# Even layer of a two-block kernel: norm applied by chunk inside its products, Fourier transforms between their groups, a ring of four mixed chunks

## The chip, the cores and the metric

The kernel runs on one core of one Trainium2 chip. The metric is the device time of one execution in microseconds; the time before is the median of three runs.

## What is computed

The reference chains two blocks of two layers each over 512 tokens of width 1024. The first block (attention, convolution, pooling, FFN) is not touched. The second block has an even layer, then an odd one; both also carry 256 context tokens, so that a row of activations is 768 wide here. What matters of the even layer, cut from the reference:

```python
hl = rmsnorm(xl, norm_pre[layer]) * (1.0 + scale_l) + shift_l      # 512 tokens
hc = rmsnorm(xc, norm_pre[layer]) * (1.0 + scale_c) + shift_c      # 256 context tokens
def proj(h, shift_fn):
    u = h @ w_in                                                   # 1024 -> 3840 columns
    s, gate_r, four, gate_f = split(u, ...)                        # 2560, 768, 256, 256
    s = s + (shift_fn(s) - s) * mu                                 # mixed with neighbours
    ...
yr = (...recurrence over s..., normed) * silu(gate_r)
yf = fourier_mix(four) * silu(gate_f)                              # fft2 over tokens and channels, real part
out = concatenate([yr, yf]) @ w_out
```

## The kernel before

All activations lie channel by channel: a tensor of width 1024 is eight chunks of 128 partitions, 768 tokens wide. A product in full precision takes both operands as a rounded part and a rest (`hi`, `lo`) and makes three matmuls per chunk (`hi·hi`, `hi·lo`, `lo·hi`), each for 256 and for 512 tokens. The column tiles of `w_in` are 30, each 128 wide (512 KB); tiles 0 to 19 are the mixed ones (18 for the recurrence, two for its small projections, called lora), 20 to 25 the gates of the recurrence, 26 and 27 the input of the Fourier mix, 28 and 29 its gates. One "group" is one tile's 48 matmuls into one of four PSUM regions.

Work is cut in stages: `stage` (L174) opens one block in which every engine has its own program, joined by semaphores, and all engines meet at its end. `Products` (from L507) is the helper of a products stage: SyncE loads weight tiles into a ring of three (L545), ScalarE makes `hi` of a tile (L565), GpSimd its `lo` (L596, the first two by VectorE), TensorE issues group after group (L1194), and `hi` and `lo` have two places each, so that tile i+2 can be rounded only when group i is done. `Ahead` lets the stage before load and split the first tiles.

The even layer (`even_layer`, L1916) runs through these stages, none of which overlaps another:

- `second_block` (L3431) loads `kept` (coefficients, 184 KB) and `xc` (context, 1 MB) and waits for both (L3441, L3442).
- `rms_norm` (L1839, by `norm_in`): ScalarE squares (L1855), TensorE sums in strips (L245), `Deviation` (L287 to L293, L253) turns the sums into the inverse root for all rows, VectorE scales (L1883), ScalarE applies gain and shift (L1863).
- `split_chunks` (L1204) makes the two parts of the normed chunks (L1212, L1218), then `serial` makes seven small tables `mus` (L1936, L1938).
- The products stage (L1950 to L1996), which starts with no weights on the chip: 30 groups in tile order by `over_tokens`, which takes all chunks for 256 tokens and then all for 512. ScalarE evacuates a group into `raw` (two places, L1945) or `gated` (L1947). VectorE mixes a raw chunk with its neighbours in seven steps (L1988, L1993) into `u`, which has all 20 chunks; ScalarE's queue sends each to HBM (L1974), and evacuating chunk m waits until chunk m-2 is mixed.
- `fourier` (L2015): loads its three tables (2.7 MB, L2030 to L2032) and waits; 12 channel products in plain fp32 (L2042), each evacuated by ScalarE (L2058) in turn with two banks; then for each of two parts the token products (L2050) and the product with the gate (VectorE, L2064).
- A stage sends the eight gate chunks to HBM (3 MB, L2002) and waits for it.
- `rwkv` (L2339) begins with a stage that loads lora, masks, small weights and the first r, k, v triple (L2367 to L2371), fills `reset`, and applies tanh to lora (L2384). Then `first_terms` (L2530) computes the terms of the first head pair with nothing beside it (L2388 the first projection), and the passes of the recurrence follow.

The odd layer's head is built in another manner, which the prediction's steps read: `residual_and_sums` (L2972) has its first weight tile loaded ahead, and `odd_products` (L3029) applies the norm chunk by chunk (L3160, L3124, L3128, L3163 and, for odd chunks, GpSimd at L3098) while TensorE takes two groups at a time through `multiply_part` as the chunks come (L3103 to L3106). `over_chunks` (L2787) is the order of matmuls used there: per chunk 256 tokens and then 512 (L2795).

## Time and profile before

| | us |
|---|---|
| median of three runs (3401.00 to 3408.59) | 3406.09 |
| the profiled execution's own time | 3404.41 |
| its span, first to last instruction | 3402.6 |
| TensorE busy | 2992.8 (88% of the span) |
| VectorE, ScalarE, GpSimd busy | 1924.0, 1167.4, 1104.5 |
| mean clock granted to TensorE | 0.939 of 2.4 GHz |

The page's busy shares are averages over all layers. The touched part lies between about 1805 and 2163 us of the span: it is read from windows of that stretch, and from timelines of single engines. In a timeline row the square bracket holds the idle time before the row and what ended it; rows that merge several instructions run from the first start to the last end, and xN counts them. A plain fp32 matmul leaves two rows.

### The profile page before, as it was taken

Reading aid. Unit: us, or ns where it says so; the run is one execution under the profiler, and the core shown is the slowest. Engines: PE = TensorE matmul, PEld = TensorE weight load, DVE = VectorE, ACT = ScalarE, POOL = GpSimd, SP = SyncE. Lnnn points to the kernel's source line nnn. Section 1 sums busy time; section 2 is a strip of 40 time slices with the busy share of each in tenths; the row PEclk is TensorE's granted clock in tenths of the full one; section 3 lists DMA queues with packets and bytes.
Section 4 is the critical chain, followed back from the end, with each engine's and each line's share of the span. In section 5 each row is a group of like instructions: output and inputs, shape, how many; then the busy total and the mean of one; then the engine's idle time right before and its main releaser. Section 6 shows DMA issues by size and latency. Waiting matters only on the chain. (4 is left out here: it accounts for less than half of the span.)

```text
span 3402.6 us, 65305 instructions
## 1 busy us (share of the span) xinstructions
PE 2992.8 (88%) x27816; PEld 2373.9 (70%) x27816; DVE 1924.0 (57%) x2634; ACT 1167.4 (34%) x2098; POOL 1104.5 (32%) x630
## 2 busy tenths in 40 slices
PE   6898988999979898899993998599999996799897
PEld 3675566887757566688772887388888894579635
DVE  3597765884159786588405760366666643353152
ACT  3223444332232344333225221244444433332222
POOL 0241133554324122355430221145445442132202
PEclk8898999999989899999996999799999998799998
DMA  9332132333233212233321331100000003132201
GB/s 365 94 90 56 32 88 68 99 93 90 72 85 94 54 38 82 69 97 95 89 79 52 109 109 58 77 17 22 22 15 10 22 9 124 44 105 81 75 13 50
DMA packets 348457, 250.33 MB, mean 74 GB/s; under 512 B 10573, under 2 KB 321539, under 8 KB 347395
## 3 DMA queue, kind: packets, MB, share of 16 engines
q1 hardware_dynamic: 341180, 232.25, 22.7%
q10 hardware_dynamic: 6980, 13.85, 1.3%
q8 instruction: 222, 3.64, 0.4%
q14 instruction: 75, 0.59, 0.1%
HBM read 223.08 MB, written 17.23 MB: 71 GB/s over the span
## 5 line engine op out<-in xcount | busy, mean ns | idle before, releaser
L596 POOL TENSOR_TENSOR weights_lo<-weights_raw,weights_hi 128x1024 fp32r<-128x1024 f32 (+1 forms) x234 | 593.3, 2536 | 1110.8 <-ACT weights_hi L565 1110.8
L1194 PE MATMUL psum<-moving_hi,weights_hi 128*128 128x512 f32 x1472 | 599.9, 408 | 73.8 <-DVE weights_lo L596 46.1
L1194 PE MATMUL psum<-moving_lo,weights_hi 128*128 128x512 f32 x1472 | 582.2, 395 | 0.0
L1194 PE MATMUL psum<-moving_hi,weights_lo 128*128 128x512 f32 x1472 | 581.3, 395 | 0.0
L1194 PEld LDWEIGHTS psum<-moving_hi,weights_hi 128*128 128x128 f32 x1472 | 281.2, 191 | 186.6 <-issue 60.1
L565 ACT ACTIVATE weights_hi<-weights_raw 128x1024 fp32r<-128x1024 f32 (+2 forms) x250 | 252.9, 1016 | 246.1 <-PE psum L1194 241.2
L1194 PEld LDWEIGHTS psum<-moving_hi,weights_lo 128*128 128x128 f32 x1472 | 281.5, 191 | 60.8
L1194 PEld LDWEIGHTS psum<-moving_lo,weights_hi 128*128 128x128 f32 x1472 | 281.9, 192 | 57.1 <-issue 3.8
L2729 POOL TENSOR_TENSOR second_off<-second_mats,second_masks 128x256 f32<-128x256 f32 x180 | 149.5, 835 | 139.9 <-PE psum L2071 139.9
L1194 PE MATMUL psum<-hn_hi,even_hi 128*128 128x256 f32 (+1 forms) x480 | 162.5, 338 | 27.3 <-DVE even_lo L596 27.3
L2720 DVE TENSOR_TENSOR second_wb<-second_wb,psum 128x512 f32<-128x512 f32 (+1 forms) x180 | 112.3, 631 | 113.7 <-PE psum L2071 112.5
L2071 PE MATMUL psum<-second_wb,second_y 64*64 64x64 f32 x2880 | 167.2, 219 | 0.1
L2795 PE MATMUL psum<-tail_hi,odd_hi 128*128 128x512 f32 (+1 forms) x384 | 143.3, 373 | 27.2 <-DVE tail_lo L2953 15.5
L1194 PE MATMUL psum<-hn_lo,even_hi 128*128 128x256 f32 (+1 forms) x480 | 162.4, 338 | 0.0
L1194 PE MATMUL psum<-hn_hi,even_lo 128*128 128x256 f32 (+1 forms) x480 | 161.9, 337 | 0.0
L744 DVE SCALAR_TENSOR_TENSOR cv<-u,columns,cv 128x512 f32<-128x512 f32 x88 | 154.9, 1760 | 3.1
L596 POOL TENSOR_TENSOR odd_lo<-odd_raw,odd_hi 128x2048 fp32r<-128x2048 f32 x19 | 88.7, 4667 | 208.8 <-ACT odd_hi L565 208.8
L596 POOL TENSOR_TENSOR even_lo<-even_raw,even_hi 128x1024 fp32r<-128x1024 f32 x28 | 67.4, 2407 | 247.9 <-ACT even_hi L565 247.9
L2071 PEld LDWEIGHTS psum<-second_wb,second_y 64*64 64x64 f32 x2880 | 138.9, 135 | 12.6 <-issue 12.3
L1194 PE MATMUL psum<-hidden_hi,weights_hi 128*128 128x512 f32 x352 | 139.7, 397 | 7.5 <-POOL weights_lo L596 7.5
L2071 PE MATMUL psum<-second_y,second_wb 64*64 64x64 f32 x2304 | 143.3, 219 | 0.0
L1735 DVE SCALAR_TENSOR_TENSOR conv<-conv_padded,columns,conv 128x512 f32<-128x512 f32 x120 | 139.2, 1160 | 3.5
(453 smaller groups left out, 6639.3 us busy)
## 6 DMA issues: line engine op xcount, KB each, us to landing
weights_raw<-in_w_up SPq DMA_DIRECT2D x88, 512.0 KB, 3.9
weights_raw<-in_w_in SPq DMA_DIRECT2D x80, 512.0 KB, 3.8
start_ada<-in_ada_w SPq DMA_DIRECT2D x12, 2048.0 KB, 16.8
odd_raw<-in_od_w_in SPq DMA_DIRECT2D x16, 1024.0 KB, 5.6
even_raw<-in_ev_w_in SPq DMA_DIRECT2D x30, 512.0 KB, 4.0
weights_raw<-in_w_down SPq DMA_DIRECT2D x32, 448.0 KB, 3.7
weights_raw<-in_w_o SPq DMA_DIRECT2D x16, 512.0 KB, 3.9
weights_raw<-in_w_down SPq DMA_DIRECT2D x16, 512.0 KB, 4.0
```

Source lines behind the costliest of these rows:

```text
L565: self.nc.scalar.activation(self.ring.hi[i % n][:, a:b], self.ring.raw[:, t % self.ring.landing, a:b], ACT.Identity)\
L596: ops.tensor_tensor(self.ring.lo[i % n][:, a:b], self.ring.raw[:, t % self.ring.landing, a:b], self.ring.hi[i % n][:, a:b].bitcast(F32), A ...
L744: nc.vector.scalar_tensor_tensor(y, x[:, 0:L], col("ffn_w", chunk), y, ALU.mult, ALU.add).then_inc(convolved, 1)
L1194: return nc.tensor.matmul(to, (hi, lo)[which][:, at:at + P], moving(k)[part], start=start and k == 0 and i == 0, stop=stop and k == n_k - ...
L1735: chain.then(nc.vector.scalar_tensor_tensor(conv[:, i, :], padded[:, i, k:k + L], col("conv_w", 2 * k + i), conv[:, i, :], ALU.mult, ALU.add))
L2071: last = nc.tensor.matmul(out[ps, :], lhsT[ps, :], rhs[ps, :], start=start, stop=stop)
L2720: V.tensor_tensor(w_, w_, bank_w(n)[:, :, 0:n_cols], ALU.add).then_inc(w_added, 1)
L2729: G.tensor_tensor(off[:, n % 2, :, :], buf.mats[:, slots(g), 0:CH], over(f"{pre_t}{LEVELS[level]}"), ALU.mult)\
L2795: return nc.tensor.matmul(region[:, a:b], (hi, lo)[which][:, at:at + P], parts[part][:, k, a:b], start=n == 0 and i == 0, stop=n == len(or ...
```

## The change

The layer becomes two stages, `even_sums` and `even_products`, and the recurrence's loading stage is gone.

`even_sums`: no stage waits for `kept` and `xc` any more. SyncE sends `xc`, weight tiles 0 and 1, `kept`, tile 2; ScalarE squares only the 512-token part, VectorE the context part; two weight tiles are split in this stage; the `mus` tables are made here; the inverse root is copied to `stats` in SBUF.

`even_products`: groups go in the order 26 to 29, 0 to 19, 20 to 25, all by `over_chunks`, with three PSUM regions (the fourth pair of banks is the Fourier mix's). The norm is applied chunk by chunk at the head while groups 0 and 1 are taken chunk by chunk. Two channel products of the Fourier mix follow each of groups 4 to 9; the token products follow groups 10 and 12. The mixed chunks go through a ring of four places (the first half of the normed chunks' room; the second half holds `z`) and 18 of them to HBM, lora stays in SBUF and gets its tanh here. Gate chunks are sent to HBM one by one (the Fourier pair together). Masks and small weights of the recurrence load here.

`rwkv` starts with `first_terms`, which now loads the first triple itself and fills `reset`.

```diff
+def even_sums(nc, sq, kept, kept_dram, h, xc, xc_dram, mus, stats, strips, at, psum, common, ahead):
+        def _(sp):
+            sp.dma_start(xc, xc_dram).then_inc(context_landed, 16)
+            for i in range(2):
+                ahead.send(sp, i)
+            sp.dma_start(kept, kept_dram).then_inc(kept_landed, 16)
+            ahead.send(sp, 2)
...
+        def _(pe):
+            for c in range(KD):
+                pe.wait_ge(squared, c + 1)
+                pe.wait_ge(context_squared, c + 1)
+                last = sum_in_strips(nc, dev.sums, common["mean_d"], sq[:, c, :], c == 0, c == KD - 1)
+            last.then_inc(dev.summed, 1)
+            dev.pe(pe)
...
+        def _(act):
+            dev.warm(strips[:, T2 // 4:T2 // 4 + 1])
+            for c in range(KD):
+                S.activation(sq[:, c, CTX:], h[:, c, :], ACT.Square).then_inc(squared, 1)
+                if c == KD - 3:
+                    ahead.hi(act, 0).then_inc(hi_made, 1)
+            ahead.hi(act, 1).then_inc(hi_made, 1)
+            dev.act(act)
+            act.wait_ge(dev.spread, 1)
+            S.activation(by_strip(stats), dev.rstd, ACT.Identity)
...
+        def _(dve):
+            dve.wait_ge(context_landed, 16)
+            for c in range(KD):
+                V.tensor_tensor(sq[:, c, 0:CTX], xc[:, c, :], xc[:, c, :], ALU.mult).then_inc(context_squared, 1)
+            dev.dve(dve)
...
+def even_products(...):
+    groups = [(i, over_chunks(nc, 0, range(KD), parts, SPLIT, P), "act") for i in range(30)]
+        s = Products(..., [(1024 * r + 1024 - T2, T2) for r in range(3)], ahead=ahead)
+        def _(sp):
+            s.load(sp, 0, 5)
...
+            sp.dma_start(seq_table, w["dft_seq"].rearrange("s (c p) f -> p s c f", p=P)).then_inc(tables_landed, 16)
...
+            s.load(sp, 5, 8)
...
+        def _(pool):
+            for c in range(1, KD, 2):
+                pool.wait_ge(rounded, c + 1)
+                nc.gpsimd.tensor_tensor(parts[1][:, c, :], hn[:, c, :], parts[0][:, c, :].bitcast(F32), ALU.subtract).then_inc(rest_pool, 1)
+            s.split_lo(pool)
...
+        def _(pe):
+            for c in range(KD):
+                pe.wait_ge(rest_pool if c % 2 else rest_dve, c // 2 + 1)
+                for g in range(2):
+                    s.multiply_part(pe, g, c, KD)
+            for g in range(2, len(groups)):
+                s.multiply(pe, g)
+                for i in channel_items(g):
+                    if i == 0:
+                        pe.wait_ge(tables_landed, 48)
+                        pe.wait_ge(s.by_act, 2)
+                    if i >= 2:
+                        pe.wait_ge(z_taken, i - 1)
+                    j, t = divmod(i, 6)
+                    PE.matmul(channel_bank(i), gated[:, 6 + j, t * P:(t + 1) * P], ch, start=True, stop=True).then_inc(by_channel, 1)
+                if g in token_after:
+                    j = token_after[g]
+                    pe.wait_ge(z_taken, 12)
+                    if j:
+                        pe.wait_ge(gate_done, j)
...
+        def _(act):
+            for c in range(KD + 1):
+                if c < KD:
+                    for i, span, _ in spans:
+                        act.wait_ge(scaled, 2 * c + i + 1)
+                        S.activation(hn[:, c, span], hn[:, c, span], ACT.Identity, bias=shift[:, i, c:c + 1], scale=gain[:, i, c:c + 1])\
+                            .then_inc(shifted, 1)
+                if c:
+                    act.wait_ge(shifted, 2 * c)
+                    S.activation(parts[0][:, c - 1, :], hn[:, c - 1, :], ACT.Identity).then_inc(rounded, 1)
+            for g in range(len(groups)):
+                if g:
+                    s.split_hi(act, g + 1)
+                act.wait_ge(s.ready, g + 1)
+                m = EVEN_TILES[g]
+                if m < 20:
+                    if m >= 2:
+                        act.wait_ge(mixed, m - 1)
+                        act.dma_start(u_dram[:, m - 2, :], u[:, (m - 2) % 4, :]).then_inc(stored[(m - 2) % 4], 16)
+                    S.activation(raw[:, m % 2, :], s.region(g), ACT.Identity).then_inc(s.by_act, 1)
...
+                for i in channel_items(g):
+                    act.wait_ge(by_channel, i + 1)
+                    S.activation(z[:, i // 6, i % 6, :], channel_bank(i), ACT.Identity).then_inc(z_taken, 1)
...
+                if m == 20:
+                    act.wait_ge(mixed, 20)
+                    S.activation(lora[:, 0, :], lora[:, 0, :], ACT.Tanh)
+                if 20 < m < 26:
+                    act.wait_ge(s.by_act, g)
+                    spill(m - 21, m - 20)
+            act.wait_ge(s.by_act, len(groups))
+            spill(5, 6)
...
+        def _(dve):
+            for m in range(20):
+                dve.wait_ge(s.by_act, mixed_at + m + 1)
+                if 4 <= m < 18:
+                    dve.wait_ge(stored[m % 4], 16 * (m // 4))
...
+                if m in (7, 9):
+                    j = (m - 7) // 2
+                    dve.wait_ge(by_token, j + 1)
+                    V.tensor_tensor(gated[:, 6 + j, :], token_out, gated[:, 8 + j, :], ALU.mult).then_inc(gate_done, 1)
...
 def rwkv(...)
-        with stage(nc, "landed tanh_ready reset_ones") as (block, sems):
...
-                self.loads = self.d == 0 and 0 < self.p < RW_PAIRS
+                self.loads = self.d == 0 and self.p < RW_PAIRS
```

## Rows read from the trace of the kernel before

**Rows 1.** Windows: stretch, length; PE, PEld, DVE, ACT, POOL busy; PEclk; DMA share, GB/s

```profile
1805.40:1850.38 44.98, 7.43 (x136) 3.54 (x137) 19.08 (x34) 24.46 (x44) 0.00 (x0) 0.54 0.21 62
1850.38:2102.47 252.09, 252.09 (x1440) 222.97 (x1440) 130.62 (x141) 51.83 (x59) 67.41 (x28) 0.99 0.28 88
2102.47:2163.01 60.54, 26.49 (x74) 14.40 (x73) 2.70 (x6) 6.29 (x15) 0.00 (x0) 0.73 0.40 152
```

**Rows 2.** Timeline of ScalarE in the even products: start us, us, engine, line, operation

```profile
1868.99 0.81 ACT L1945 ACTIVATE raw<-psum 128x768 f32<-128x768 f32 x1 [6.58 <-PE psum L1194]
```

**Rows 3.** SyncE's timeline, and DMA issues of that stretch: count, size, us to landing

```profile
1807.00 0.34 SPq L3441 DMA_DIRECT2D second_kept<-kept_spill  x1
...
second_xc<-context_spill SPq DMA_DIRECT2D x1, 1024.0 KB, 4.9
```

**Rows 4.** Timeline of TensorE in the odd layer: one chunk's sums in strips

```profile
2963.60 0.87 PE L245 MATMUL psum<-tail_room,table 128*32 128x192 f32 x8 [1.18 <-ACT tail_room L3010]
```

**Rows 5.** Timeline of VectorE from the last sums of the odd norm to its products' head

```profile
2964.53 0.36 DVE L287 TENSOR_SCALAR tail_room<-psum 128x192 f32<-128x192 f32 x1 [1.56 <-PE psum L245]
...
2968.92 1.90 DVE L3160 TENSOR_TENSOR tail_room<-h,tail_room 128x512 f32<-128x512 f32 x3 [2.25 <-PEq L183]
```

**Rows 6.** Timelines of ScalarE and VectorE in the even norm and split, by groups

```profile
1823.12 2.73 DVE L1883 TENSOR_TENSOR second_mixed_in<-second_xc,psum 128x256 f32<-128x256 f32 x8 [0.73 <-PE psum L253]
1823.57 9.68 ACT L1863 ACTIVATE second_mixed_in<-second_mixed_in,second_kept 128x256 f32<-128x256 f32 x16 [2.57 <-DVE second_mixed_in L1883]
...
1833.52 5.97 ACT L1212 ACTIVATE hn_hi<-second_mixed_in 128x768 fp32r<-128x768 f32 x8 [0.27 <-PEq L183]
1834.39 7.04 DVE L1218 TENSOR_TENSOR hn_lo<-second_mixed_in,hn_hi 128x768 fp32r<-128x768 f32 x8 [3.76 <-ACT hn_hi L1212]
```

**Rows 7.** Timeline of TensorE at two starts of odd products

```profile
2972.46 0.80 PE L2795 MATMUL psum<-tail_hi,odd_hi 128*128 128x512 f32 x1 [4.71 <-DVE tail_lo L3163]
...
2977.22 0.39 PE L2795 MATMUL psum<-tail_hi,odd_lo 128*128 128x512 f32 x1
...
3001.43 0.80 PE L2795 MATMUL psum<-tail_hi,odd_hi 128*128 128x512 f32 x1 [2.73 <-POOL odd_lo L596]
...
3004.50 0.40 PE L2795 MATMUL psum<-tail_lo,odd_hi 128*128 128x512 f32 x1
```

**Rows 8.** Timelines of VectorE and GpSimd, the same stretch of the odd layer

```profile
2980.84 8.25 DVE L3166 TENSOR_TENSOR tail_room<-second_xc,tail_room 128x256 f32<-128x256 f32 x8
...
2982.60 4.87 POOL L596 TENSOR_TENSOR odd_lo<-odd_raw,odd_hi 128x2048 fp32r<-128x2048 f32 x1 [0.52 <-ACT odd_hi L565]
```

**Rows 9.** Groups of instructions by form: the split of one even weight tile

```profile
L596 POOL TENSOR_TENSOR even_lo<-even_raw,even_hi 128x1024 fp32r<-128x1024 f32 x28 | 67.4, 2407 | 247.9 <-ACT even_hi L565 247.9
```

**Rows 10.** Timeline of TensorE in products taken by chunk, two chunk starts six apart

```profile
2920.82 0.28 PE L2795 MATMUL psum<-tail_hi,odd_hi 128*128 128x256 f32 x1
...
2927.11 0.28 PE L2795 MATMUL psum<-tail_hi,odd_hi 128*128 128x256 f32 x1
```

**Rows 11.** Timeline of TensorE in the Fourier stage: token products of the first part

```profile
2123.74 1.99 PE L2050 MATMUL psum<-second_dft_ctx,second_z 128*128 128x256 f32 x8 [0.47 <-ACT second_z L2058]
...
2132.44 1.89 PE L2050 MATMUL psum<-second_dft_ctx,second_z 128*128 128x256 f32 x8
```

**Rows 12.** Timelines of VectorE and ScalarE around one mixed chunk

```profile
1895.88 6.03 DVE L1993 SCALAR_TENSOR_TENSOR second_mixed_in<-raw,mus,second_mixed_in 128x255 f32<-128x255 f32 x6
...
1902.35 0.33 ACTq L1974 DMA_DIRECT2D mixed_spill<-second_mixed_in  x1
```

**Rows 13.** DMA issues of whole kernel: count, size, median us to landing

```profile
mixed_spill<-second_mixed_in ACTq DMA_DIRECT2D x20, 384.0 KB, 2.3
second_rkv<-mixed_spill SPq DMA_DIRECT2D x6, 1152.0 KB, 6.2
```

**Rows 14.** Timelines of VectorE and ScalarE in the recurrence's first terms

```profile
2166.87 1.76 DVE L2472 TENSOR_TENSOR_SCAN second_cum<-second_reset,second_sg 128x768 f32<-128x768 f32 x1 [3.25 <-ACT second_sg L2441]
...
2172.80 0.84 ACT L2451 ACTIVATE second_e<-second_cum 128x768 f32<-128x768 f32 x1
```

More of the change, by code:

```diff
@@ L2532, in first_terms, with _ @@
                 terms = Terms(sems, 0)
+                @block.sync
+                def _(sp):
+                    terms.load(sp)
                 @block.tensor
```

373 lines of the change are left out of this document (112 added, 261 removed).

## The prediction, as put on record before the changed kernel ran

> **What bounds the kernel now.** I read the page's shares first, then windows over the touched part, then timelines of single engines. TensorE is busy for 88% of the span, so what is worth finding is time in which it stands still, or work on it that something else sets. The windows cut the layer in three [rows 1]. From the end of the block before (1805.40) to the first product (1850.38) there are 45.0 us in which TensorE works 7.4: loads, norm, split, tables and the first weights come one behind another. From there to 2102.47 it works 252.09 of 252.09 us at a clock of 0.99: this stretch is bound by TensorE alone. From 2102.47 to the recurrence's first instruction at 2163.01 there are 60.5 us with 26.5 of TensorE: tables, Fourier mix, a 3 MB store and a load stage in a row. Group 1 is done just before its evacuation at 1868.99 [rows 2], say 1868.95, so 28 groups take (2102.47 - 1868.95) / 28 = 8.34 us each.
>
> So 105.5 us surround the products. The change puts most of it beside TensorE, but the Fourier products stay TensorE's own work and only move into its busy stretch. The sum has three parts, all against the profiled execution: 3404.41 us, 1.68 below the median of 3406.09; its span is 3402.6, with 1.8 around it.
>
> **Up to the products' stage.** The first load leaves at 1807.0 as before; now it is `xc`, which lands 4.9 us after issue [rows 3]: 1811.9. ScalarE's 512-token squares don't wait for it; VectorE's context squares, of the shape of the context scalings, take about 2.73 / 8 = 0.34 us each [rows 6]. TensorE's sums of one chunk of 768 tokens cost 0.87 us at the low clock [rows 4]; back to back I take 0.75, so eight chunks from 1812.3 end at 1818.0 to 1818.5. That is later than the last square (six squares, `hi` of tile 0 behind its landing at about 1813.5, two squares: 1815.6), so ScalarE's two weight splits hide behind the sums; if the tile lands 3 us later they no longer do, and each further us counts. In the odd layer VectorE's first step behind the sums starts at 2964.53 and its products' head at 2968.92 [rows 5], 4.4 us with the stage's change between. The same steps are here, the `mus` tables fit beside the copy of the root. Head starts at H = 1822.4 (bounds 1821 and 1825).
>
> **The head, groups 0 and 1.** Per chunk ScalarE needs two shifts, 9.68 / 8 = 1.21 us, and one rounding, 5.97 / 8 = 0.75 [rows 6]: 1.96, so 15.7 for eight. VectorE needs 0.63 (1.90 / 3 [rows 5]) and 0.34 per chunk, and 7.04 / 8 = 0.88 for every second [rows 6]: 11.3. GpSimd makes four rests of 768 columns, by width 0.75 of 2.41 us [rows 9]: 7.2. The first chunk is ready after three chunks' scaling, one rounding and one rest, about H + 4.9. TensorE's pace by chunk is 6.29 / 6 = 1.05 us per group [rows 10], 2.10 for two groups, 16.8 for eight chunks at the full clock. It will start at 1.2 GHz: in the odd head that lasted from 2972.46 to 2977.22, where a matmul's row falls from 0.80 to 0.39 [rows 7]: 4.8 us of which half is lost. So group 1 is done at H + 4.9 + 16.8 + 2.4 = H + 24.1 = 1846.5. The last chunk must be there 2.1 us earlier, at H + 22. With all engines side by side it is there at about H + 18.
>
> VectorE and GpSimd don't run side by side freely: eight context scalings took 8.25 us while one `odd_lo` of 4.87 ran [rows 8], against 2.73 for the same shape alone. The Trainium skill, SBUF — State Buffer, section Terms, says why: the two share a port pair that one takes for a whole instruction while the other fully blocks. By that rule the two engines' work adds up, 11.3 + 7.2 = 18.5, plus some 2 of start: the last chunk at H + 20.5. The trace agrees with it, and it speaks against this head: it leaves 1.5 us of room instead of 4.
>
> **The stall behind the head.** Both `hi` places are in use until groups 0 and 1 end, and these now end 1.05 us apart. So tile 2 is rounded only when group 0 is done: evacuation 0.81 [rows 2], `hi` 0.75 x 4 / 3 = 1.0 by width, `lo` 2.41 [rows 9], hand-offs 0.1: 4.3 us, less the 1.05 of group 1: TensorE stands 3.3 us. In the odd products a wait of 2.73 us was followed by half clock from 3001.43 to 3004.50 [rows 7], 1.5 lost; I take 1.5 (bounds 0 and 2.4). Group 2 in effect starts at 1846.5 + 3.3 + 1.5 = 1851.3 instead of 1868.95: **17.6 us less**.
>
> **The middle.** Chunk order: 8 x 1.05 = 8.39 instead of 8.34, 28 times: +1.4. Twelve channel products: 24 rows at 1.99 / 8 = 0.25 us, as plain fp32 rows of that width take [rows 11]: 6.0. Each pair finds both banks taken a group earlier, so no wait. Token products: 2132.44 - 2123.74 = 8.70 us per part [rows 11], 17.4 for two. The second part waits for the first gate product, behind the mixing of chunk 7: one mix ends at 1901.91 and the next group is done by 1902.35 [rows 12], 0.44 us of room, and the gate product is 0.96: 0.5 of stall (0 and 1.5). The tables (2.7 MB) stand in SyncE's queue before tile 5, but are sent some 60 us before group 4's products ask for them. Ring of four: chunk m waits for the store of m-4, sent two groups earlier and landed in 2.3 us [rows 13]; hidden by 16.8 us, and without that cover each group would wait for a landing. Three PSUM regions: an evacuation is done some 1.3 us into the next group, hidden. The SyncE queue's late loads (masks, small weights) have over 150 us. ScalarE gets seven stores, twelve copies of half an evacuation and tanh in a stretch in which it is busy 51.8 of 252 us. Together **+25.3 us**.
>
> **The tail.** Behind the last group: evacuation 0.8, last store landing 2.3 [rows 13], waits and the stage's change 0.6: the recurrence's first stage starts 3.7 us after TensorE, against 60.54 before. In it the triple now loads beside the projection: 6.2 us to landing [rows 13] and some 0.7 of VectorE for `kk` (between the 0.34 and 0.88 of VectorE in [rows 6]), so the scan starts 6.9 after the stage's start instead of 2166.87 - 2163.01 = 3.9. But the exponentials started only at 2172.80 [rows 14], 9.8 after the stage's start, when the scan (1.76) and its difference (0.9) had been done at 6.6: 3.2 us of room for 3.0. I take 0.3 (bounds 0 and 3). **56.5 us less.**
>
> **Sum.** -17.6 + 25.3 - 56.5 = -48.8: 3355.6 for an execution like the profiled one, 3357.3 for the median: **3357**.
>
> **Rivals.**
> 1. *The head is bound by its chunks.* The room of 1.5 us is gone (a rest on GpSimd slower, ScalarE kept by its hand-offs); TensorE stops between chunks and stays longer at 1.2 GHz, where a chunk costs 4.2. For: the blocking in [rows 8]. Against: the odd head, built alike, went to full clock in 4.8 us. Four more chunks at half clock are +8.4, with a late last chunk +10: 3367. Chance 0.15.
> 2. *The Fourier insertions cost waits.* Each of the eight places where TensorE changes between products and Fourier work costs a hand-off of about 1 us (late copy of `z`, gate product behind a late mix): +8: 3365. For: room of only 0.44 us in rows 12. Against: copies of 0.4 against a group of 8.4. Chance 0.10.
> 3. *The gaps close better.* The stall doesn't lower the clock (1.5), `xc` lands sooner when first and alone and the sums run at their narrow shape's rate (2), the gate product waits for nothing (0.5), group 1's tail hides more (2): 3351. Chance 0.14.
> 4. *Slower: mixing sets the pace.* Place: VectorE's loop over 20 chunks, now behind evacuation, ring store and gate product. It decides from 8.39 us per chunk; to lose the whole gain it must take 48.8 / 20 = 2.4 more, 10.8. A store landing more than 16.8 us after issue, or GpSimd's `lo` blocking all of it over again (6.7 + 2.4 = 9.1, not enough), would be wanted; at 11.5 us per chunk the time is 3357 + 20 x 3.1 = 3419. For: the blocking in [rows 8]. Against: the mix already runs beside `lo` and ends within the group [rows 12]. Chance 0.02.
> 5. *The change doesn't do what it says*, that is, the norm or the transforms aren't hidden: the Fourier products never were (they are in the sum), and stages fewer is certain. If the head's overlap failed whole, with loads and norm as long as before, 17.6 is lost: 3374. Chance 0.01.
>
> **How the numbers follow.** The forecast has 0.58. The range takes rivals 1 to 3 in and the bounds of the unknown costs: 3347 (rival 3 with the low ends of the tail and the start) to 3370 (rival 1 with the tail's 3). About 0.2% of 3406, 7 us, is what a measurement of this kernel can tell from no change; only rival 4 comes near or above it: faster 0.97, same 0.01, slower 0.02.
>
> **What would show it.** In the profile after: `stats` copied at about 1822; products' first matmul near 1827, chunk starts 2.1 us apart once the clock is up; one TensorE wait of about 3.3 us on GpSimd's `lo` before group 2; groups 8.4 us apart, 9.3 with channel products, 17.1 with token products; a window of the products stage busy all but 5 us; first terms' first projection 3.7 us behind the last product, at about 2113. I am wrong if group 1 ends after 1855, if mixed chunks are more than 8.5 us apart without Fourier work between, or if the recurrence's passes change in length.

## The result: 1.5% faster, and where the time went

The changed kernel takes 3352.28 us (median of four runs, 3348.69 to 3356.36) against 3403.55 for the kernel before in the same sitting (3399.52 to 3408.59): a ratio of 0.985, 95% interval 0.9835 to 0.9864. Forecast were 3357, range 3347 to 3370. The profiled execution took 3348.69, its span is 3346.9.

| us | before | after |
|---|---|---|
| profiled execution, span | 3404.41, 3402.6 | 3348.69, 3346.9 |
| end of the block before (VectorE's last step, taken as the layer's start) | 1805.39 | 1802.89 |
| from there to the first product | 44.99 | 21.82 |
| to the end of the last product | 297.08 | 305.58 |
| to the recurrence's exponentials, as in [rows 14] | 367.41 | 318.98 |
| from the exponentials to the end of the span | 1229.8 | 1225.03 |
| TensorE busy, clock granted | 2992.8, 0.939 | 2986.4, 0.948 |

The touched layer, by the two marks that both kernels have, is 48.4 us shorter; the sum of the forecast was 48.8. The other 7.3 us of the 55.7 between the two profiled executions lie ahead of the layer and behind it, where nothing was changed; the first experiment asks what they are.

The three parts of the layer changed like this. The first product comes 23.2 us sooner after the layer's start, the stretch of products is 31.7 us longer in place (283.76 against 252.09), and the time from the last product to the exponentials fell by 56.9 us. Before, the latter began with these rows of TensorE:

```profile
2114.16 9.11 PE L2042 MATMUL psum<-second_dft_channels,second_gated 128*128 128x256 f32 x24 [11.68 <-DMA second_dft_ctx<-in_dft_ctx]
...
2163.01 2.90 PE L2388 MATMUL psum<-second_lora,second_w 64*128 64x256 f32 x4 [21.81 <-PEq L183]
```

That is 11.7 us of waiting for the tables, 27.0 from the first Fourier product to the end of the last, and 21.8 of store and loads; 3.9 us are left of it.

Windows of the changed kernel, which answer to [rows 1] (columns as there): up to the first product, the two groups by chunk, the other products with the Fourier work, the end of the stage, the recurrence's first 9.5 us.

```profile
1802.89:1824.71 21.82, 5.96 (x73) 3.67 (x73) 9.23 (x26) 11.81 (x20) 4.67 (x2) 0.58 0.63 180
1824.71:1844.40 19.69, 19.17 (x96) 16.41 (x96) 10.63 (x13) 13.12 (x20) 8.02 (x4) 0.88 0.39 138
1844.40:2108.46 264.06, 260.81 (x1416) 221.81 (x1416) 131.07 (x142) 53.73 (x70) 67.05 (x28) 0.99 0.28 91
2108.46:2112.34 3.88, 0.00 (x1) 0.00 (x0) 0.00 (x0) 0.82 (x2) 0.00 (x0) 1.00 0.50 203
2112.34:2121.87 9.53, 6.69 (x11) 3.12 (x12) 4.48 (x7) 5.10 (x6) 0.00 (x0) 0.52 0.38 124
```

TensorE now stands still for 16 us ahead of its first product, 3.2 inside and 3.9 behind, and works in all the rest. The waits of TensorE between 1820 and 2113, with the total us, the times and the longest:

```profile
PE psum L2716 <- DVE hn_lo L1965: 6.5, 1, 6.5
PE psum L2310 <- PEq L183: 3.9, 1, 3.9
PE psum L2716 <- POOL even_lo L596: 3.2, 1, 3.2
PE psum L1908 <- DVE second_gated L1986: 0.6, 1, 0.6
```

These are the four that the prediction named: the head's first chunk, the change of stage behind the last gate store, the split of tile 2, and the gate product. There is no fifth. The sums stage runs as forecast too; from its timelines (VectorE's context squares, TensorE's sums, the copy of the root, the first step of the head):

```profile
1804.50 0.34 SPq L1789 DMA_DIRECT2D second_xc<-context_spill  x1
...
1809.46 2.77 DVE L1827 TENSOR_TENSOR second_gated<-second_xc 128x256 f32<-128x256 f32 x8 [6.56 <-DMA second_xc<-context_spill]
...
1810.03 5.34 PE L245 MATMUL psum<-second_gated,table 128*32 128x192 f32 x64 [18.63 <-DVE second_gated L1827]
...
1818.30 0.81 ACT L1821 ACTIVATE second_raw<-psum 128x768 f32<-128x768 f32 x1 [2.12 <-PE psum L253]
...
1819.70 0.69 DVE L1962 TENSOR_TENSOR second_mixed_in<-h,second_raw 128x512 f32<-128x512 f32 x1 [1.30 <-PEq L183]
```

The first square on `xc` starts 5.0 us after its load was issued, the sums take 0.67 us a chunk (0.75 forecast), and the head starts 16.8 us behind the block before (17.0 forecast).

What did differ from the forecast stands in TensorE's timeline behind the head:

```profile
1824.71 0.58 PE L2716 MATMUL psum<-hn_hi,even_hi 128*128 128x256 f32 x1 [6.47 <-DVE hn_lo L1965]
...
1847.10 0.58 PE L2716 MATMUL psum<-hn_hi,even_hi 128*128 128x256 f32 x1 [3.22 <-POOL even_lo L596]
...
1852.17 0.63 PE L2716 MATMUL psum<-hn_lo,even_hi 128*128 128x512 f32 x1
...
1853.50 0.40 PE L2716 MATMUL psum<-hn_hi,even_hi 128*128 128x512 f32 x1
...
1858.40 0.28 PE L2716 MATMUL psum<-hn_hi,even_hi 128*128 128x256 f32 x1
```

A matmul of 512 columns has a row of 0.63 us until about 1853 and of 0.40 behind it: 6.1 us at half clock behind the wait. Group 2, from 1847.10 to 1858.40, takes 11.30 us; in two profiles whose clock stays up behind the same wait (gates_at_end and rests_on_dve below) it takes 8.51. So 2.8 us are lost. The term in the sum was 1.5, its upper bound 2.4.

### The profile page after: what moved, and what is told of

Read it like the earlier page. It is cut to its first block and busy times, and to the rows that moved or that the text cites. A ratio compares the mean times of both kernels' runs of the same rounds, so it can differ in the third digit from the quotient of the medians.

```text
span 3346.9 us, 65146 instructions
## 1 busy us (share of the span) xinstructions
PE 2986.4 (89%) x27752; PEld 2368.6 (71%) x27752; DVE 1922.6 (57%) x2636; ACT 1164.4 (35%) x2091; POOL 1115.7 (33%) x636
## 5 line engine op out<-in xcount | busy, mean ns | idle before, releaser
L2716 PE MATMUL psum<-hn_hi,even_hi 128*128 128x256 f32 x480 | 166.7, 347 | 9.7 <-DVE hn_lo L1965 6.5
L2716 PE MATMUL psum<-hn_lo,even_hi 128*128 128x256 f32 x480 | 164.9, 344 | 0.0
L2716 PE MATMUL psum<-hn_hi,even_lo 128*128 128x256 f32 x480 | 163.3, 340 | 0.0
L755 DVE SCALAR_TENSOR_TENSOR h<-h,psum 128x512 f32<-128x512 f32 x16 | 11.0, 688 | 228.4 <-PE psum L1150 228.4
```

What stands on the lines that cost most here:

```text
L755: nc.vector.scalar_tensor_tensor(h[:, m, :], h[:, m, :], ALPHA, s.region(g), ALU.mult, ALU.add).then_inc(s.by_dve, 1)
L2716: return nc.tensor.matmul(region[:, a:b], (hi, lo)[which][:, at:at + P], parts[part][:, k, a:b], start=n == 0 and i == 0, stop=n == len(or ...
```

## How the experiments are read

Medians of one kernel move by 2 or 3 us from one measurement to the next and the intervals are 0.3% wide, so steps of 1 to 6 us are read from the profiles. I take three lengths from each: **layer** (the layer's start to the exponentials), **products** (first product's start to last product's end, with the Fourier work between), and **half clock** (the time in that stretch in which rows have their long form, at the head and behind the wait for tile 2). "Net" is the products less half of their half-clock time. Half is a little too much: a chunk's six matmuls take 1.92 us at half clock (1849.19 to 1851.11 in the changed kernel) and 1.05 at full, so that 0.45 of such a stretch is lost. The last column takes off 0.45.

| kernel | median us | ratio to before | layer | products | half clock: head, behind wait | net | at 0.45 |
|---|---|---|---|---|---|---|---|
| changed | 3352.28 | 0.985 | 318.98 | 283.76 | 4.6, 6.1 | 278.4 | 278.9 |
| after_again | 3352.08 | 0.9851 | 317.95 | 282.95 | 3.6, 5.5 | 278.4 | 278.8 |
| head_order | 3346.69 | 0.9838 | 312.78 | 278.53 | 6.1, 0 | 275.5 | 275.8 |
| hi_first | 3351.60 | 0.9840 | 317.14 | 282.47 | 5.9, 3.4 | 277.8 | 278.3 |
| serial_head | 3363.21 | 0.9880 | 325.86 | 276.75 | 3.1, 0 | 275.2 | 275.3 |
| no_fourier | 3331.76 | 0.9787 | 294.52 | 260.11 | 6.1, 3.5 | 255.3 | 255.8 |
| gates_at_end | 3359.90 | 0.9863 | 321.78 | 280.43 | 3.5, 0 | 278.7 | 278.8 |
| load_stage | 3360.05 | 0.9865 | 324.27 | 283.10 | 5.9, 3.5 | 278.4 | 278.8 |
| token_order | 3351.22 | 0.9845 | 312.58 | 278.51 | 2.7, 0 | 277.1 | 277.3 |
| rests_on_dve | 3348.65 | 0.9838 | 315.46 | 280.34 | 3.2, 0 | 278.8 | 278.9 |
| ring_of_two | 3355.05 | 0.9855 | 320.44 | 284.89 | 4.7, 6.1 | 279.5 | 280.0 |
| all_three | 3347.86 | 0.9836 | 310.98 | 276.01 | 3.6, 0 | 274.2 | 274.4 |
| all_four | 3346.71 | 0.9828 | 310.92 | 275.36 | 4.6, 0 | 273.0 | 273.3 |

Net repeats to 0.1 us in three kernels whose products are the same (changed, after_again, load_stage), to 0.4 with the two others (gates_at_end, rests_on_dve). At 0.45 all five agree to 0.1, so the 0.4 came from the halving.

## Experiments

### The same kernel again

> The changed kernel once more, unaltered. The touched layer is 48.4 us shorter between its marks in the two traces, yet the profiled executions differ by 55.7 and the medians by 51.3. Theory 'the rest is variation from execution to execution' (mine): the ratio comes out between 0.9845 and 0.9865, and in this profile the parts outside the layer that were shorter (first block -2.5 us, recurrence and odd layer together -4.8 us) differ from those of before by other amounts, their sum nearer to -2. Rival 'the change also makes code outside the layer shorter' (other addresses, other DMA timing): the same parts are shorter by the same 7.3 us again, within 1 us.

Measured: ratio 0.9851, 0.9836 to 0.9866. The layer starts at 1804.76 instead of 1802.89, and behind the exponentials the span goes on for 1227.89 instead of 1225.03: the 7.3 us have shrunk to 2.5 (0.6 and 1.9) with nothing changed. Over the thirteen profiles of this case that have the new layer the start lies between 1802.17 and 1809.00, mean 1805.2 (before: 1805.39), and the rest between 1225.03 and 1233.99, mean 1229.6 (before: 1229.8). So the one profile of before lies at the mean of the thirteen, and the 7.3 us were variation of single executions. The rival is out. It also says that a difference of two profiled executions can be off by 7 us in this kernel; the layer between its marks varies by far less.

### The stall behind the head: order of the first two groups

```diff
-            for c in range(KD):
-                pe.wait_ge(rest_pool if c % 2 else rest_dve, c // 2 + 1)
-                for g in range(2):
-                    s.multiply_part(pe, g, c, KD)
+            for g, c in ((0, 0), (1, 0), (0, 1), (1, 1), (0, 2), (1, 2), (0, 3), (0, 4), (1, 3), (0, 5), (0, 6), (0, 7),
+                         (1, 4), (1, 5), (1, 6), (1, 7)):
+                if g == 0:
+                    pe.wait_ge(rest_pool if c % 2 else rest_dve, c // 2 + 1)
+                s.multiply_part(pe, g, c, KD)
```

> Only the order of the parts of groups 0 and 1 at the head changes: group 0 is finished some 4.2 us ahead of group 1, so tile 2 can be rounded and split while TensorE still works. Theory 'the stall behind the head is the split of tile 2, and the half clock after it is a consequence of the stall' (mine): the 3.22 us wait goes to at most 0.3, the clock stays up at 1847 (3.0 us back), some 0.6 us of new waiting for chunks early in the head; -5.8 us against the changed kernel. Rival 'the head is bound by the arrival of its chunks': group 0 alone reaches each chunk sooner, the wait only moves from behind the head into it; 0 to -2 us. Rival 'the clock falls there anyway': the wait goes, the half clock stays, -2.8.

Measured: net 275.5 against 278.4, and no half clock behind the head; layer 312.78 against 318.98 and 317.95, so 5.7 less than their mean; median 5.4 below the unaltered kernel beside it. ScalarE's timeline shows why (evacuation of group 0, then `hi` of tile 2, each twice):

```profile
1842.08 0.81 ACT L1938 ACTIVATE second_gated<-psum 128x768 f32<-128x768 f32 x1 [3.42 <-PE psum L2717]
1842.78 1.05 ACT L565 ACTIVATE even_hi<-even_raw 128x1024 fp32r<-128x1024 f32 x1
1846.28 0.81 ACT L1938 ACTIVATE second_gated<-psum 128x768 f32<-128x768 f32 x1 [2.44 <-PE psum L2717]
1846.98 1.05 ACT L565 ACTIVATE even_hi<-even_raw 128x1024 fp32r<-128x1024 f32 x1
```

Group 0 is evacuated 4.2 us ahead of group 1 instead of 1.65, and the split of tile 2 (4.3 us) fits beside group 1's last chunks. The first rival is out: TensorE has no wait over 0.3 us in the head. The clock did not fall either; one profile says little of that, since the next experiment shows the same wait without a fall, but the clock stays up in all four kernels that lack the wait. The room that the prediction gave to the head was there.

### The size of the wait and the clock: tile 2 rounded ahead of the evacuation

```diff
-                if g:
+                if g > 1:
                     s.split_hi(act, g + 1)
                 act.wait_ge(s.ready, g + 1)
+                if g == 0:
+                    s.split_hi(act, 2)
```

> ScalarE rounds tile 2 before it evacuates group 0 instead of after. Both theories: the wait of 3.22 us behind the head shrinks by one evacuation of 0.8 to about 2.4 or 2.5. Theory 'any wait of that size brings the clock down' (the odd head's wait of 2.73 us was followed by half clock): -0.7 to -1 us against the changed kernel, with half clock for some 4 to 6 us after the wait. Rival 'there is a size of wait between 1.75 and 2.73 us under which the clock stays' : -3.7 us, and full clock after the wait.

Measured: the wait is 2.61 us, net 277.8, 0.6 less. TensorE's rows behind it:

```profile
1848.59 0.39 PE L2718 MATMUL psum<-hn_hi,even_hi 128*128 128x256 f32 x1 [2.61 <-POOL even_lo L596]
...
1849.31 0.63 PE L2718 MATMUL psum<-hn_lo,even_hi 128*128 128x512 f32 x1
...
1852.94 0.39 PE L2718 MATMUL psum<-hn_lo,even_hi 128*128 128x512 f32 x1
```

So the shorter wait was followed by half clock as well, for 3.4 us. But my theory that a wait of this size brings it down each time is wrong. Eight profiles have the same wait of 3.22 us, from the same instruction, between the same groups; the half clock behind it lasted 6.1, 5.5, 3.5, 0, 3.5, 0, 0 and 6.1 us. Windows of 6.0 us from the end of this wait, of the changed kernel, of load_stage, and of gates_at_end (whose edits touch nothing here):

```profile
1847.10:1853.10 6.00, 6.00 (x19) 5.13 (x20) 0.00 (x0) 0.47 (x1) 2.28 (x1) 0.50 0.60 175
```

```profile
1848.09:1854.09 6.00, 6.00 (x26) 5.26 (x27) 0.00 (x0) 0.47 (x1) 2.28 (x1) 0.72 0.60 175
```

```profile
1850.51:1856.51 6.00, 6.00 (x35) 5.29 (x36) 0.00 (x0) 0.47 (x1) 2.29 (x1) 1.00 0.61 175
```

ScalarE, GpSimd and the DMA share are alike; the clock is 0.50, 0.72 and 1.00, and TensorE gets through 19, 26 or 35 recorded matmuls. The price of this wait's clock, read from the length of group 2, is between 0 and 2.8 us from one execution to the next, 1.4 on average of the eight.

One thing in the table goes with it: how long the half clock at the head had lasted, which had ended some 15 us before the wait began. In the three of the eight with the shortest (2.7 to 3.5 us) the clock stayed up; in the next three (3.6, 4.6 and 4.7) it was down for 5.5 to 6.1 us; in the two with the longest (5.9 and 6.1) for 3.5, and hi_first, with 5.9, for 3.4. So the two stretches hang together; why, and what sets the first, no experiment here shows. The four kernels without a wait there (head_order, serial_head, all_three, all_four) show full clock.

### What the overlap is worth

```diff
-            for c in range(KD):
-                pe.wait_ge(rest_pool if c % 2 else rest_dve, c // 2 + 1)
-                for g in range(2):
+            pe.wait_ge(rest_pool, KD // 2)
+            pe.wait_ge(rest_dve, KD // 2)
+            for g in range(2):
+                for c in range(KD):
                     s.multiply_part(pe, g, c, KD)
```

> TensorE waits for all eight chunks, then takes group 0 whole and group 1 whole, instead of chunk by chunk. Theory 'overlapping products with the chunks is worth what the chunks take' (mine): the first product comes 14.2 us later; group 0 and group 1 take 16.8 us plus some 2.3 at the low clock; tile 2 is split in the shade of group 1, so that the 3.2 us of wait and the 3.0 us of low clock behind it are gone: +8.1 us against the changed kernel, of which the overlap alone is 14.2. Rival 'the chunks come sooner when TensorE is not beside them': last chunk clearly earlier than H + 19.25, and the result below +6.

Measured: TensorE waits 20.6 us instead of 6.5, the first product comes 35.40 us into the layer instead of 21.82 and 21.30, 13.8 later; net is 3.2 less (3.5 at 0.45), about the stall of 3.22; the layer is 7.4 longer than the mean of the two unaltered profiles (318.5). The last rest ends 19.1 us behind the head's start, as in the changed kernel (19.25), so TensorE's work beside them does not slow the chunks, and the rival is out. The median is 11 us higher; the layer explains 7.4 of the 11, and the rest stays unexplained, though this profile's layer starts late (1809.00, the latest of all).

Of the 23.2 us by which the first product comes sooner than before the change, the overlap is thus 13.8. The other 9.4 (no wait for `kept` and `xc` in a stage of their own, weights loaded and split ahead, the tables `mus` beside other work, fewer stages) are not told apart by any experiment.

### Fourier work left out

```diff
-        channel_items = lambda g: range(2 * (g - 4), 2 * (g - 4) + 2) if 4 <= g < 10 else ()
-        token_after = {10: 0, 12: 1}
+        channel_items = lambda g: ()
+        token_after = {}
...
-                    V.tensor_tensor(gated[:, 6 + j, :], token_out, gated[:, 8 + j, :], ALU.mult).then_inc(gate_done, 1)
+                    V.tensor_tensor(gated[:, 6 + j, :], gated[:, 6 + j, :], gated[:, 8 + j, :], ALU.mult).then_inc(gate_done, 1)
```

> Leaves out the Fourier mix's twelve channel products, the copies of their results and the token products; the gate is multiplied with the untransformed input instead, so that the gate products and stores stay. Theory 'the Fourier mix costs TensorE its own length and nothing besides' (mine): the layer, from the end of the block before to the recurrence's exponentials, is shorter than in the changed kernel by 5.1 for the channel products, 17.2 for the token products and 0.6 for the wait on the gate: -22.9 us, within 0.7. Rival 'the insertions cost hand-offs or slow the mixing': the gain is larger, -25 or more. Rival 'something else is late in their place' (mixing, tile loads): less than 21 us is gained and new waits stand on TensorE.

Measured: net 255.3 against 278.4, 23.1 less, and no new wait. Groups are 8.40 us apart where channel products follow them at 9.25. The Fourier mix costs TensorE its own length; the eight changes between the two kinds of work, which rival 2 of the prediction priced at 1 us each, cost the 0.55 us on the gate product and nothing else.

### Stores and loads in the tail

gates_at_end sends the gates in one store behind the last group:

```diff
-                if m == 10:
-                    act.wait_ge(gate_done, 2)
-                    spill(6, 8)
...
-                if 20 < m < 26:
-                    act.wait_ge(s.by_act, g)
-                    spill(m - 21, m - 20)
...
-            spill(5, 6)
+            act.wait_ge(gate_done, 2)
+            spill(0, 8)
```

> All eight gate chunks go to HBM in one store behind the last group, instead of one by one as they are ready. Theory 'only the last store lies in the open' (mine): the wait between the last product and the first terms grows from 3.9 us to about 10.3, since 3 MB landed 8.7 us after issue in the kernel before against 2.3 for one chunk: +6.4 us, nothing else moves. Rival 'the end of the products stage is bound by something else' (tail of the small loads, the lora's tanh): +3 or less. Rival 'stores beside the products cost them bandwidth': the products stage gets shorter by over 1 us without them.

load_stage gives the first triple a stage again:

```diff
-                self.loads = self.d == 0 and self.p < RW_PAIRS
+                self.loads = self.d == 0 and 0 < self.p < RW_PAIRS
...
+        with stage(nc, "landed") as (block, sems):
+            @block.sync
+            def _(sp):
+                sp.dma_start(rkv[:, :, :], triple(0)).then_inc(sems[0], 16)
+                sp.wait_ge(sems[0], 16)
```

> The first r, k, v triple gets a stage of its own again between the products and the first terms. Theory 'the triple's landing is hidden by the first projections' (mine): 6.2 us to landing and 0.4 for the change of stage come into the open; the scan no longer waits for the triple, but the exponentials then come 9.5 to 9.8 us behind the first terms' start as before: +6.6 us. Rival 'the exponentials are held up by the triple too': the exponentials come earlier in their stage by 2 or 3 us, so the total is +4 or less.

Measured: the wait ahead of the first terms is 10.13 us in gates_at_end and 10.42 in load_stage, against 3.91. TensorE's first row of the recurrence in each:

```profile
2119.22 2.04 PE L2305 MATMUL psum<-second_lora,second_w 64*128 64x256 f32 x3 [10.13 <-PEq L183]
```

```profile
2118.63 2.90 PE L2316 MATMUL psum<-second_lora,second_w 64*128 64x256 f32 x4 [10.42 <-PEq L183]
```

That is +6.2 and +6.5 with 6.4 and 6.6 expected; net is 278.7 and 278.4, so the small stores cost the products nothing that can be seen. In load_stage the scan no longer waits for the triple, yet the exponentials start 9.80 us into the stage, as they did before the change (9.79) and as they do with the triple's load beside them (9.50 and 9.79). VectorE's and ScalarE's timelines of the changed kernel:

```profile
2118.25 0.62 DVE L2392 TENSOR_SCALAR second_kk<-second_rkv,second_kept 128x768 f32<-128x768 f32 x1 [4.64 <-DMA second_rkv<-mixed_spill]
2118.79 1.75 DVE L2394 TENSOR_TENSOR_SCAN second_cum<-second_reset,second_sg 128x768 f32<-128x768 f32 x1
...
2118.92 0.90 ACT L2366 ACTIVATE second_a<-psum,second_kept 128x768 f32<-128x768 f32 x1 [3.01 <-PE psum L2310]
2120.57 0.96 DVE L2398 TENSOR_TENSOR second_e<-second_cum,second_sg 128x768 f32<-128x768 f32 x1
2120.57 1.28 ACT L2373 ACT_TABLE_LOAD   x1
2121.87 0.84 ACT L2373 ACTIVATE second_e<-second_cum 128x768 f32<-128x768 f32 x1
```

The exponentials need the scan and the difference behind it (L2398), which is done at 2121.53. ScalarE is never idle after 2118.92: it comes to them at 2121.87, behind a square and a table load of 1.28 us. So the triple is hidden, with 0.34 us to spare, and 0.33 to 0.68 in all profiles that have its load beside the first terms, against 3.2 without it.

### The order inside a group

```diff
-    groups = [(i, over_chunks(nc, 0, range(KD), parts, SPLIT, P), "act") for i in range(30)]
+    by_chunks = [over_chunks(nc, 0, range(KD), parts, SPLIT, P) for i in range(30)]
+    by_tokens = lambda made: [made[6 * c + 3 * side + i] for side in range(2) for c in range(KD) for i in range(3)]
+    groups = [(i, by_tokens(made) if i > 1 else made, "act") for i, made in enumerate(by_chunks)]
```

> Groups 2 to 29 take all chunks for 256 tokens and then all for 512, as in the kernel before; groups 0 and 1 stay by chunk. Theory 'the order by chunk costs 0.06 us per group' (from 8.40 us between evacuations against 8.34 before): -1.6 us over 28 groups. Rival 'the 0.06 comes from Fourier work, stores and loads beside the products': 0, groups stay 8.40 apart.

Measured: evacuations follow each other in 8.34 us in this kernel,

```profile
2021.45 0.81 ACT L1937 ACTIVATE second_raw<-psum 128x768 f32<-128x768 f32 x1 [6.58 <-PE psum L2718]
2029.79 0.81 ACT L1937 ACTIVATE second_raw<-psum 128x768 f32<-128x768 f32 x1 [6.58 <-PE psum L2718]
```

and in 8.40 in the changed one:

```profile
2024.87 0.81 ACT L1935 ACTIVATE second_raw<-psum 128x768 f32<-128x768 f32 x1 [6.64 <-PE psum L2716]
2033.27 0.81 ACT L1935 ACTIVATE second_raw<-psum 128x768 f32<-128x768 f32 x1 [6.64 <-PE psum L2716]
```

Net is 1.3 less, and 1.6 less at 0.45 (1.6 expected). Without any half clock to take off, from group 2's first product to the last product's end: 256.94 us here, 258.58 in gates_at_end and rests_on_dve, 1.6 less. The order by chunk costs that, and only the first two groups need it.

### GpSimd beside VectorE at the head

```diff
-            for c in range(1, KD, 2):
-                pool.wait_ge(rounded, c + 1)
-                nc.gpsimd.tensor_tensor(parts[1][:, c, :], hn[:, c, :], parts[0][:, c, :].bitcast(F32), ALU.subtract).then_inc(rest_pool, 1)
...
-                pe.wait_ge(rest_pool if c % 2 else rest_dve, c // 2 + 1)
+                pe.wait_ge(rest_dve, c + 1)
...
-                if c >= 2 and c % 2 == 0:
+                if c >= 2:
```

> The four rests that GpSimd makes at the head of the products go to VectorE. Theory 'the head is set by TensorE's work and the split of tile 2, the blocking of VectorE by GpSimd is paid in the room' (mine): the two long scalings of VectorE (2.05 and 2.34 us instead of 0.42 and 0.68) go back to their usual length, and the time from the first product to the last, without what half clock took, stays at 278.4 within 0.5. Rival 'blocking costs time': chunks come sooner and over 1 us is gained. Rival 'VectorE alone is slower than the two': 0.96 more per odd chunk makes the last chunk late and TensorE waits at the head, over 1 us lost.

The changed kernel, VectorE and GpSimd at the head (a scaling of 256 columns, one of 512, and the two rests beside them):

```profile
1825.18 0.42 DVE L1962 TENSOR_TENSOR second_mixed_in<-second_xc,second_raw 128x256 f32<-128x256 f32 x1
1825.51 0.68 DVE L1962 TENSOR_TENSOR second_mixed_in<-h,second_raw 128x512 f32<-128x512 f32 x1
1826.11 2.05 DVE L1962 TENSOR_TENSOR second_mixed_in<-second_xc,second_raw 128x256 f32<-128x256 f32 x1
...
1829.90 2.34 DVE L1962 TENSOR_TENSOR second_mixed_in<-h,second_raw 128x512 f32<-128x512 f32 x1
...
1825.67 2.21 POOL L1881 TENSOR_TENSOR hn_lo<-second_mixed_in,hn_hi 128x768 fp32r<-128x768 f32 x1 [8.58 <-ACT hn_hi L1925]
1829.62 2.07 POOL L1881 TENSOR_TENSOR hn_lo<-second_mixed_in,hn_hi 128x768 fp32r<-128x768 f32 x1 [1.73 <-ACT hn_hi L1925]
1834.40 1.85 POOL L1881 TENSOR_TENSOR hn_lo<-second_mixed_in,hn_hi 128x768 fp32r<-128x768 f32 x1 [2.71 <-ACT hn_hi L1925]
```

VectorE's steps of 0.42 and 0.68 last 2.05 and 2.34 when a rest of GpSimd's started ahead of them; they end 0.3 and 0.5 us behind it. The rule weighed in the prediction (the Trainium skill, SBUF — State Buffer, section Terms) describes this. Measured with the edit: all scalings at 0.42 and 0.68, the last rest 17.4 us behind the head's start instead of 19.25, and net 278.8 against 278.4. So the blocking is real, and sharing the rests between the two engines makes the last chunk 1.8 us later than giving them all to VectorE; the time of this kernel doesn't depend on it (278.9 at 0.45 with and without): TensorE's work sets the head.

### How near mixing is to the pace

```diff
-                        act.dma_start(u_dram[:, m - 2, :], u[:, (m - 2) % 4, :]).then_inc(stored[(m - 2) % 4], 16)
+                        act.dma_start(u_dram[:, m - 2, :], u[:, m % 2, :]).then_inc(stored[m % 2], 16)
...
-                if 4 <= m < 18:
-                    dve.wait_ge(stored[m % 4], 16 * (m // 4))
+                if 2 <= m < 18:
+                    dve.wait_ge(stored[m % 2], 16 * (m // 2))
```

> The mixed chunks go through two places instead of four, so that VectorE waits for the landing of the store of chunk m-2, issued just ahead of the evacuation of chunk m. Theory 'a landing of 2.3 us, issued 1.2 before VectorE asks, costs VectorE 1.1 us of the 1.72 in which it stood idle anyway' (mine): VectorE's idle time per chunk turns into a wait for the store, groups stay 8.40 apart, total 0 to +0.5 us. Rival 'mixing is near enough to the pace that it takes over' (the slower-than-before case of the prediction): chunks over 8.6 apart, +4 us or more. It tells how near mixing is to setting the pace.

Measured: net +1.1, more than the 0.5 expected. Groups stay 8.40 apart; all of it is one wait. TensorE's waits of this kernel, and VectorE's:

```profile
PE psum L2716 <- POOL even_lo L596: 3.2, 1, 3.2
PE psum L1908 <- DVE second_gated L1986: 1.7, 1, 1.7
...
DVE second_mixed_in L1973 <- DMA mixed_spill<-second_mixed_in: 52.6, 16, 12.3
```

VectorE waits for a store at 16 chunks and TensorE doesn't notice, but at the one place where TensorE wants something of VectorE in the same group, the gate product behind the mix of chunk 7, it waits 1.71 instead of 0.55. I had counted the late mix as hidden and forgotten what is queued behind it. The slower-than-before rival is far away all the same: a ring half as deep costs 1.1 us, not the 48.8 that it needs.

### A version that combines them

The edits of head_order and token_order, and the second token part one group later, when its gate product is done:

```diff
-        token_after = {10: 0, 12: 1}
+        token_after = {10: 0, 13: 1}
```

> Three edits to the changed kernel together: group 0 ahead of group 1 at the head (measured alone: 3.0 us, and no half clock behind it), groups 2 to 29 by tokens (alone: 1.3 us), and the second token part after group 13 instead of 12, so that the gate product is there (0.6). Theory 'they add up, since all three lie on TensorE's own chain' (mine): from the first product to the last, without what half clock took, 273.5 against 278.4 us; with the half clock that the changed kernel showed in its two profiles the layer is 7.5 to 8 us shorter than there, median about 3344.5. Rival 'they overlap': under 4 us without the clock. For the half clock: mine, that it goes with the wait, shows full clock at 1847; a half-clock stretch there without a wait would speak against it.

Measured: net 274.2, 4.2 less where 4.9 were expected (4.5 at 0.45, where the three edits alone come to 3.1, 1.6 and 0.6); layer 310.98, 7.5 below the mean of the two unaltered profiles; full clock behind the head. The wait on the gate product is gone. What is short of the sum is in the head, where TensorE now waits for GpSimd's rests:

```profile
PE psum L2719 <- DVE hn_lo L1968: 6.5, 1, 6.5
...
PE psum L2719 <- POOL hn_lo L1883: 0.6, 2, 0.3
```

In this order group 0 asks for the late chunks sooner; head_order had no such waits over 0.3, but it spent 6.1 us at half clock there, all_three 3.6, and a faster TensorE reaches them earlier. That is argued from one profile each. So here the earlier rests should pay, and all_four adds the edit of rests_on_dve:

> The three edits of the run before, and VectorE makes all rests of the head. Theory 'in the new order of the head TensorE does run into its chunks, which it did not in the old one' (mine): the two waits of 0.29 and 0.34 us on GpSimd's rests at the head go, and what is short of the sum of the three edits comes back: from the first product to the last, without what half clock took, 273.5 against 274.2 with three. Rival 'the earlier rests are worth nothing here either': 274.2 again, with other waits in the head. For the half clock: no wait over 1 us stands behind the head, and mine says full clock there once more. Median within 2 us of the run before, which the medians can't tell apart; the trace does.

Measured: net 273.0, 1.2 less (0.7 expected), no wait in the head, and full clock behind it once more. The same edit that was worth nothing in the changed kernel is worth about 1 us in this one. Median 3346.71, ratio to before 0.9828, 0.9813 to 0.9842: 5.4 us below the unaltered kernel's second measurement. Those two intervals overlap (0.9836 to 0.9866), so that it beats the changed kernel rests on the layers of the profiles, 310.92 against 318.98 and 317.95; that it beats the kernel before is certain. Nor do medians tell it from head_order alone (3346.69, layer 312.78).

## Why the prediction was right, point by point

- **Up to the products' stage.** Right: head 16.8 us behind the block before, 17.0 forecast. In the other profiles the first product comes 20.7 to 21.9 us into the layer (21.9 forecast; serial_head left aside), so the term was up to 1.2 us too long.
- **The head.** Right: first product 5.0 us into it (4.9), 2.10 us per chunk, group 1 done 24.2 us in (24.1). Half clock lasted 4.6 us in this profile (4.8 forecast), 2.7 to 6.1 in all of them. The last chunk was there at 19.25, midway between the 18 of engines that don't disturb each other and the 20.5 of engines whose work adds up: only two of GpSimd's four rests held up a step of VectorE's. Rival 1 is out: TensorE has no wait between its chunks, and in rests_on_dve chunks that come 1.8 us sooner gain nothing.
- **The stall.** Its length was right (3.22 against 3.3), and head_order shows that its cause was too. The step that failed is the low clock behind it: 1.5 us in the sum with a bound of 2.4, read from one wait of the odd layer; 2.8 in this profile, 0 to 2.8 over eight. That the 1.5 is near their mean of 1.4 is luck: one row had been taken for a rule.
- **The middle.** +25.3 forecast; measured from group 2's first product, less its lost clock, to the last product's end 258.6 us against 28 groups of 8.34, that is +25.1. Channel products were mis-sized: 0.85 per pair, 5.1 in all, where I took 6.0 from rows that overlap each other. Token parts 8.6 each (8.7). Chunk order +1.7 by the intervals, 1.6 by experiment (1.4). Gate stall 0.55 (0.5). No wait for tables, `z` or stores: rival 2 is out by no_fourier.
- **The tail.** 3.9 us to the first terms (3.7); then 9.5 to the exponentials where 10.1 were forecast. The 0.3 for the triple's load was not there; load_stage's 9.80 says that it costs nothing. The room of 0.2 us that the forecast left for it (3.2 against 3.0) measured 0.34.
- **The sum.** -16.6, +25.1 and -56.9, together -48.4, for -17.6, +25.3 and -56.5: errors of 1.0, 0.2 and 0.4. The first, the lost clock, was in good part made up by the other two.
- **The range.** Its upper end adds up. Its lower end doesn't quite: rival 3's 3351 less the low ends of the tail (0.3) and the start (1.4) is 3349, not 3347.
- **The median.** 3352.28 was measured, 4.7 below 3357. Some 2.5 of that is the base: the 3406.09 that the sum was taken from is a median of three runs; with four it came out at 3403.55, and later between 3403.3 and 3405.6. The layer of the six profiles with the same groups in the same order (changed, after_again, gates_at_end, load_stage, rests_on_dve, ring_of_two), less the edits' own 6.2, 6.5 and 1.1, is 317.5 us on average, 49.9 below before, which gives another 1.1. The last 1.1 us is less than the medians repeat to. The figure lies near rival 3's 3351, but mostly not for its reasons: `xc` landed no sooner and the gate product was waited for. Two came in part: the sums ran at 0.67 us a chunk instead of 0.75, and the stall left the clock up in three of eight profiles.

## What to carry to other kernels

When a chain of loads, norm and split is taken into a products stage, write down when each weight tile's place comes free: two groups that end together leave the next tile's split in the open, and finishing one of them a few chunks ahead hid it here at no cost that can be seen. Late work that is hidden from one consumer may not be hidden from the next thing in its queue; look for the one place where another engine wants something behind it. And measure a change of 1 to 6 us in a 3400 us kernel between two marks of the trace around the touched part, not by the execution's total, which moves by as much by itself.

## What was not expected of the hardware

- The same wait of TensorE, 3.22 us long, was followed by half clock for 0, 3.5, 5.5 or 6.1 us in different executions, with the same work around it. The Trainium skill, TensorE: Matmul & The Clock Gate, section What's actually happening, says that the clock is set by how busy TensorE has been; the trace agrees in that every fall here had an idle TensorE ahead of it. With equal idleness ahead, whether it fell and for how long went with the length of the half clock at the head (the hi_first experiment); what lies behind that no run here shows.
- The head started from the same idleness each time (6.5 us; 20.6 in serial_head) and stayed at half clock for 2.7 to 6.1 us.
- A rest of 768 columns takes GpSimd 2.21 and 2.07 us where VectorE is in a step of its own when it starts, and 1.85 where it isn't; a step of VectorE that meets one ends when it does, up to 1.7 us late.
